# A hybrid mixer and ConvFFN layer on one Trainium2 core: the mixers' projections as pairs with seven half-width block products for eight, the values first, feed-forward operands loaded early

## The chip, the core and the metric

The kernel runs as one program on one core of a Trainium2 chip. Its time is the device time of one execution in microseconds (us); the median of several runs is compared. A core has TensorE (PE, matmuls), VectorE (DVE), ScalarE (ACT), GpSimd (POOL) and SyncE (SP), which here issues all the DMA transfers. Each engine works through its own queue in order, and semaphores tie the queues together.

## The reference, cut to what matters

One layer over 2048 prompt positions and 64 sample positions, all in float32, with D = 1024:

```python
def mixer(xn, ...):
    z = xn @ w_in
    bg, cg, h, q, k, v, gr, r = jnp.split(z, SPLITS, axis=-1)   # 512,512,512,256,256,512,16,512
    cv, conv_new = causal_dwconv(cg * h, conv_prev, conv_w)     # 3 taps
    y_conv = rmsnorm(bg * cv, g_conv)
    logg = jax.nn.log_sigmoid((gr @ w_alpha + b_alpha)) / GATE_TAU
    ...                                                         # q scaled by HEAD_K ** -0.5
    o, gla_new = gla(q, k, v, logg, gla_prev)                   # gated linear attention, chunks of 64
    y_gla = rmsnorm(o, g_gla) * jax.nn.silu(r)
    y = jnp.concatenate([y_conv, y_gla], axis=-1) @ w_out
def conv_ffn(xn, prev, w_up, conv_w, w_down):
    uc, new = causal_dwconv(xn @ w_up, prev, conv_w)            # 1024 -> 2 * 2816, 3 taps
    a, g = jnp.split(uc, 2, axis=-1)
    return (jax.nn.silu(g) * a) @ w_down, new
x = x + mixer(rmsnorm(x)); x = x + conv_ffn(rmsnorm(x)); y = rmsnorm(x)
```

## The kernel before

Positions are the columns of PE's moving operands. They lie in three blocks: 768, 768, and 512 prompt positions with a gap of two and the 64 sample positions (580 columns in all). Half a block is 384, 384 or 290 columns (HALF, CMAX is the largest), and a block has 6, 6 and 5 token tiles of 128 (TILES). A float32 product is made of three matmuls (`product`, L1429; lines L1434 to L1436): every operand is split into a high part, which ACT copies in PE's rounding, and a low part, which is the subtraction raw − high; high·high, high·low and low·high are summed in PSUM.

All three blocks go through the mixer first, then all through the feed-forward part. For each block:

- **Norm and transposes.** Token tiles are normed (x_n), transposed on PE (`turn_1`) and split into xt_hi (ACT) and xt_lo (DVE): 8 k-tiles by the block's columns.
- **First stage ("z").** A unit is 128 output columns of w_in, 512 KB, loaded into one of four slots of `raw`; ACT writes its high part (`high_unit`, L478), POOL its low part (`low_unit`, L485). There are 4 units of r, the gate gr (32 rows, w_gr), and 4 of q and k. Each is computed in two chunks, 256 and 512 (324) columns wide (Z_CHUNKS), in PSUM banks in turn; ACT reads each bank (`read_group`). SiLU of r is applied in gla_y right after the r units.
- **Values.** v_tok is computed by token tile, 24 matmuls of 512 columns each, with the normed positions as weights' side; the weights lie in all four slots. ACT reads them (L1220).
- **Convolution stage.** 12 units (cg, h, bg for j = 0 to 3), each 2 × 24 matmuls of half a block. ACT reads cg into conv_y, DVE multiplies h by it into conv_u, applies three taps, and multiplies by bg. Between these 24 products `mix_events` (L488) deals the steps X, Y and Z of each token tile's linear attention evenly: X makes the state's addends and the output of the first chunk and the next tile's gate, Y the second chunk and the gate's cumulative sum, Z the mean squares and the next tile's scores. Between X and Y, DVE brings the state on (gla_s) and ACT and DVE make the log gate lg, for which PE waits in Y.
- **Out-projection** in four passes p = 0 to 3 over the token tiles, summed on DVE into resid (`add_out`); in pass 3 the second norm and the transposes of the feed-forward operands of this block and of the first norm of the next block run along. The feed-forward operands go to DRAM: parts of the positions (xs_a, xs_b) as x_ops (ops_stored) and four sums of them, made on DVE in tst, from block 0 and 1 (sums_stored).

The feed-forward part has 22 steps for each block. Its up-projections already run as Strassen-Winograd products: a pair of 128-column units as a 2 × 2 block matrix (k halves × units) against the positions as 2 × 2 blocks (k halves × column halves) needs seven half-width products for eight. Sums of the weights (`sum_up`: four of 128 × 512 on DVE), copies on ACT (`high_up`, into slots of wq) and lows on POOL (`low_up`, L906) precede them; r_1, r_2, r_3 are partial results in SBUF. The operands on the positions' side are loaded raw as xo_raw, copied high and subtracted low, 4 × 384 columns each (DVE L1839 in block 0, ACT L1038). In block 0 the split weights are stored to w_ops (L598) for the other blocks.

Each engine's program is written out in order; a load on SP waits until its slot is free, and whatever stands behind it in SP's queue waits too.

## Time and profile before

| | |
|---|---|
| median of 3 runs | 2422.65 us (2420.15 to 2423.34) |
| the profiled execution | 2420.94 us, span 2419.2 us, granted clock 0.992 |
| PE busy | 2320.1 us, 96% |
| DVE, ACT, POOL busy | 1586.5 us, 975.5 us, 1142.3 us |
| mixers of the three blocks, from the timeline | about 18 to 958 us |
| feed-forward part | about 958 us to the end |

A timeline's row gives the start, the length, the engine, the line and the operation, output<-inputs with their shapes, and how many like instructions follow each other (x4). In brackets stands the engine's idle time just before it and the instruction that ended it.

### The profile page before, as it was taken

The numbers are of one execution on the slowest core, as the hardware profiler recorded it, in microseconds if no ns is written. First come the engines' busy times: TensorE is split into PE (matmuls) and PEld (weight loads), VectorE is DVE, ScalarE is ACT, GpSimd is POOL, SyncE is SP. The second block draws the span as 40 slices with busy tenths as digits, with TensorE's granted clock in tenths as the row PEclk, the third lists the DMA queues.
The fourth block names the chain that finished last, engine by engine and source line by source line (L and its number), as shares of the span: only waits on it lengthen the run. The fifth ranks groups of instructions, "written<-read, shape, count | busy, mean of one in ns | idle before, by whom it ended". The sixth has DMA issues, their size and how long they took to land. (4 is left out here: it accounts for less than half of the span.)

```text
span 2419.2 us, 38967 instructions
## 1 busy us (share of the span) xinstructions
PE 2320.1 (96%) x12962; PEld 2113.1 (87%) x12962; DVE 1586.5 (66%) x2397; ACT 975.5 (40%) x1881; POOL 1142.3 (47%) x1117
## 2 busy tenths in 40 slices
PE   7999999999999999799999998999999988999997
PEld 6889878899788987799999998899999987999996
DVE  2046662155650656698988988667667677878886
ACT  4333353333353435444444445333333335444443
POOL 3222323222423334778878785444444445455552
PEclk9999999999999999899999999999999999999999
DMA  5111335111452234744444457644444456555553
GB/s 158 59 53 44 122 114 172 50 44 42 151 183 78 79 120 147 272 170 150 162 173 147 165 175 258 206 160 144 141 160 150 139 183 231 196 191 191 186 195 106
DMA packets 257550, 355.01 MB, mean 147 GB/s; under 512 B 12189, under 2 KB 195314, under 8 KB 257458
## 3 DMA queue, kind: packets, MB, share of 16 engines
q1 hardware_dynamic: 257457, 353.77, 43.8%
q8 instruction: 59, 0.97, 0.2%
q14 instruction: 34, 0.27, 0.0%
HBM read 276.54 MB, written 77.19 MB: 146 GB/s over the span
## 5 line engine op out<-in xcount | busy, mean ns | idle before, releaser
L1434 PE MATMUL ps<-xo,wq 128*128 128x384 f32 (+1 forms) x1848 | 599.7, 324 | 27.6 <-issue 12.0
L1435 PE MATMUL ps<-xo,wq 128*128 128x384 f32 (+1 forms) x1848 | 598.6, 324 | 0.0
L1436 PE MATMUL ps<-xo,wq 128*128 128x384 f32 (+1 forms) x1848 | 598.0, 324 | 0.0
L2089 DVE TENSOR_TENSOR resid<-resid,ps 128x512 f32<-128x512 f32 (+1 forms) x728 | 477.2, 680 | 76.1 <-PE ps L1436 45.3
L485 POOL TENSOR_TENSOR w_lo<-raw,w_hi 128x512 fp32r<-128x512 f32 x192 | 251.4, 1337 | 566.5 <-ACT w_hi L478 566.5
L906 POOL TENSOR_TENSOR wq<-wu_raw,wq 128x256 fp32r<-128x256 f32 x396 | 378.2, 978 | 118.2 <-ACT wq L1018 118.2
L1434 PEld LDWEIGHTS ps<-xo,wq 128*128 128x128 f32 x1848 | 350.4, 190 | 50.5 <-issue 28.0
L1435 PEld LDWEIGHTS ps<-xo,wq 128*128 128x128 f32 x1848 | 351.0, 190 | 20.1
L1436 PEld LDWEIGHTS ps<-xo,wq 128*128 128x128 f32 x1848 | 351.3, 190 | 0.0
L1434 PE MATMUL ps<-xt_hi,w_hi 128*128 128x384 f32 (+4 forms) x960 | 316.7, 330 | 7.9 <-DVE xt_lo L1807 3.7
L2106 DVE SCALAR_TENSOR_TENSOR up_y<-up_u,params,up_y 128x768 f32<-128x768 f32 (+1 forms) x264 | 287.3, 1088 | 50.2 <-ACT up_y L1062 31.5
L1435 PE MATMUL ps<-xt_hi,w_lo 128*128 128x384 f32 (+4 forms) x960 | 310.1, 323 | 0.0
L1436 PE MATMUL ps<-xt_lo,w_hi 128*128 128x384 f32 (+4 forms) x960 | 310.1, 323 | 0.0
L1434 PE MATMUL ps<-wd_hi,hid_hi 128*128 128x512 f32 x704 | 276.8, 393 | 11.7 <-DVE resid L2089 11.6
L1436 PE MATMUL ps<-wd_lo,hid_hi 128*128 128x512 f32 x704 | 277.3, 394 | 0.0
L1435 PE MATMUL ps<-wd_hi,hid_lo 128*128 128x512 f32 x704 | 274.7, 390 | 0.0
L936 POOL TENSOR_TENSOR wd_lo<-wd_raw,wd_hi 128x512 fp32r<-128x512 f32 x132 | 174.7, 1345 | 157.0 <-ACT wd_hi L1097 157.0
L1434 PEld LDWEIGHTS ps<-xt_hi,w_hi 128*128 128x128 f32 x960 | 182.2, 190 | 20.1 <-issue 8.8
L930 POOL TENSOR_TENSOR hid_lo<-up_y,hid_hi 128x384 fp32r<-128x384 f32 (+1 forms) x132 | 120.2, 932 | 165.2 <-ACT hid_hi L1090 165.2
L906 POOL TENSOR_TENSOR wq<-wu_sum,wq 128x256 fp32r<-128x256 f32 x176 | 158.6, 926 | 64.7 <-ACT wq L1018 63.7
L1435 PEld LDWEIGHTS ps<-xt_hi,w_lo 128*128 128x128 f32 x960 | 182.3, 190 | 5.4 <-issue 0.5
L1436 PEld LDWEIGHTS ps<-xt_lo,w_hi 128*128 128x128 f32 x960 | 182.0, 190 | 5.1
(207 smaller groups left out, 3499.2 us busy)
## 6 DMA issues: line engine op xcount, KB each, us to landing
wq<-w_ops SPq DMA_DIRECT2D x176, 512.0 KB, 4.4
wu_raw<-in_w_up_dram SPq DMA_DIRECT2D x89, 512.0 KB, 4.1
w_ops<-wq SPq DMA_DIRECT2D x88, 512.0 KB, 2.7
raw<-in_w_in_dram SPq DMA_DIRECT2D x72, 512.0 KB, 3.9
wd_raw<-in_w_down_dram SPq DMA_DIRECT2D x66, 512.0 KB, 5.1
x_in<-in_x_prompt_dram SPq DMA_DIRECT2D x32, 512.0 KB, 4.5
raw<-in_w_out_dram SPq DMA_DIRECT2D x24, 512.0 KB, 3.4
wu_raw<-in_w_up_dram SPq DMA_DIRECT2D x43, 256.0 KB, 3.1
```

The lines of the kernel that those rows point to most:

```text
L485: last = pool.tensor_tensor(w_lo[:, s, r], raw[:, s, r], w_hi[:, s, r].bitcast(F32), ALU.subtract)
L906: last = pool.tensor_tensor(wq[:, WQ_AT[i], 1, r], src[:, r], wq[:, WQ_AT[i], 0, r].bitcast(F32), ALU.subtract)
L930: last = pool.tensor_tensor(hid_lo[:, par, r], up_y[:, 0, r], hid_hi[:, par, r].bitcast(F32), ALU.subtract)
L936: last = pool.tensor_tensor(wd_lo[:, par, r], wd_raw[:, r], wd_hi[:, par, r].bitcast(F32), ALU.subtract)
L1434: pe.matmul(out, lh, rh, start=(first and n == 0), stop=False, skip_group_check=skip)
L1435: pe.matmul(out, ll, rh, start=False, stop=False, skip_group_check=skip)
L1436: last = pe.matmul(out, lh, rl, start=False, stop=end, skip_group_check=skip)
L2089: last = dve.tensor_tensor(resid[0:m, t, s], resid[0:m, t, s], ps[0:m, bank, :], ALU.add)
L2106: dve.scalar_tensor_tensor(y, up_u[:, m, tap:tap + w], params[:, FFN_TAP + tap, bass.ds(m * NF + f, 1)], y, ALU.mult, ALU.add).then_inc(su ...
```

## The change

It alters the mixers of all three blocks and the hand-over to the feed-forward part; the 66 feed-forward steps stay, apart from the first one's loads.

1. **Values first.** In each block the values are computed straight after the norm, tile 0 and 1 in two halves by weight slots, then the gate product in two chunks of half a block.
2. **Pairs.** r, q and k, cg, h and bg are computed as ten pairs of units (PAIRS), each in seven products of 12 matmuls on half a block (`pair_product`), by the feed-forward part's scheme and with its buffers wu_raw, wu_sum, wq and its semaphores (STEPS = 30 counts lie ahead of the feed-forward part's). Operands 0, 2, 5, 6 are quarters of xt_hi and xt_lo; 1, 3 and 4 are sums of quarters: t_2 and t_3 (DVE) and t_1 (POOL). Operand 5's quarter is also replaced: DVE writes a sum (n4, in xt_raw, which lies over xt_lo's second part) and ACT and DVE split it in place, after the values and the gate product have read the old one.
3. Per pair DVE makes four weight sums, r_2, r_3m and three quarters of the output (four where h and bg are multiplied in), ACT seven copies of weights, r_1 and one quarter, POOL seven lows of 2 × 256 columns; DVE makes the lows 2 and 4 of pairs 1 to 3. For cg, h and bg two convolution rows are handled at once (conv_u0, conv_u1).
4. **Attention steps** begin after product 2 of pair 4; the first tile's gate, sums and scores stand behind products (1, 6), (3, 1) and (4, 2), and 5 products come after the last step. The factor 1/8 of q moves from ACT's read into a DVE operation of each tile. SiLU of r comes after product 2 of pair 2.
5. **Start of the feed-forward part.** Operands 0 to 2 of the positions are loaded at the start of the last block's out stage, 3 and 4 in its middle, 5 and 6 ahead of the last stores to x_ops; their splitting on ACT and DVE moves up as well, and so does the first step's weights'. load_up(0, 1) no longer waits for the stores.
6. Buffers move in SBUF to make place; the parameters' rows are transposed in pair 0 of block 0 instead of in the norm.

```diff
+PAIRS = [("r", 0), ("r", 2), ("qk", 0), ("qk", 2)] + [(kind, j) for j in (0, 2) for kind in ("cg", "h", "bg")]
...
+AT_GATE, AT_SUMS, AT_SCORES = (1, 6), (3, 1), (4, 2)
...
+LEFT = 5
+LOW_PAIRS, LOW_OPS = (1, 2, 3), (2, 4)
...
+        def pair_operand(b, i, part):
+            c = HALF[b]
+            if i in (1, 3, 4):
+                return {1: t_2, 3: t_3, 4: t_1}[i][:, part, :, 0:c]
+            k, c0 = {0: (0, 0), 2: (4, 0), 5: (0, c), 6: (4, c)}[i]
+            return (xt_hi, xt_lo)[part][:, k:k + 4, c0:c0 + c]
```

Order of work (`mix_events`), the loads on SP and the first loads for the feed-forward part:

```diff
-            groups = [(j, m, c) for j in range(CJ) for m in range(3) for c in range(len(CHUNKS[b]))]
+            products = [(p, i) for p in range(NPAIR) for i in range(NP)]
             steps = [(s, t) for t in range(TILES[b]) for s in ("XYZ" if tile_cols(b, t)[1] == P else "XZ")]
-            out, g = [], 0
+            out, g = [], products.index(AT_SCORES) + 1
+            for p, i in products[:g]:
+                out.append(("G", p, i))
+                if (p, i) in (AT_GATE, AT_SUMS, AT_SCORES):
+                    out.append(({AT_GATE: "P", AT_SUMS: "S", AT_SCORES: "C"}[p, i], 0))
+            rest = len(products) - g - LEFT
...
-                upto = (n + 1) * len(groups) // len(steps)
-                while g < upto:
-                    out.append(("G",) + groups[g])
-                    g += 1
-            return out
+                upto = len(products) - LEFT - rest + (n + 1) * rest // len(steps)
+                out += [("G",) + product for product in products[g:upto]]
+                g = upto
+            return out + [("G",) + product for product in products[g:]]
...
+            def load_pair(b, p, part):
+                n = (A11, A21)[part]
+                sp.dma_start(wu_raw[:, n:n + 2, :].rearrange("p n (k c) -> p (n k) c", c=P),
+                             pair_source(p, part)).then_inc(mix_sems[f"w_loaded{part}"], 16)
...
+                unit_free(sp, (0, 1), unit_index(b, "v", 0, 0) + 1)
+                for p in range(NPAIR):
+                    for part in range(2):
+                        if p:
+                            pair_split(sp, NPAIR * b + p - 1, (2, 5)[part])
+                        load_pair(b, p, part)
...
+                if b == NB - 1:
+                    sp.wait_ge(ops_stored, 16 * 3 * b)
+                    sp.wait_ge(sums_stored, 16 * 4 * b)
+                    mix.wait(sp, "p_done", NP * NPAIR)
+                    for i in range(3):
+                        load_x_op(0, i)
+                for n in range(4, 8):
+                    load_unit(sp, out_unit(b, n))
...
-                    sp.wait_ge(ops_stored, 16 * 3 * b)
+                    mix.wait(sp, "out_done", 4 * nt)
+                    for i in range(3, 5):
+                        load_x_op(0, i)
+                    unit_free(sp, (0, 1), unit_index(NB, "v", 0, 0))
                     load_up(0, 0)
...
-                    mix.wait(sp, "out_done", 4 * nt)
-                    for i in range(3):
-                        if i == 2:
...
-                    for i in range(3, 5):
+                    for i in range(5, NP):
                         load_x_op(0, i)
...
-                    sp.wait_ge(ops_stored, 16 * (3 * NB + 1))
-                    for i in range(5, NP):
-                        load_x_op(0, i)
...
+                    sp.wait_ge(ops_stored, 16 * (3 * NB + 1))
                     load_down(0)
```

POOL's t_1 and ACT's order at the start of the pairs:

```diff
+                n1.wait(pool, "lo", 2 * nt)
+                wait(pool, sums_stored, 16 * 4 * b)
...
+                for step, (left, left_part, right, right_part, op) in enumerate([
+                        (xt_hi, c, xt_hi, 0, ALU.subtract), (None, 0, xt_lo, c, ALU.add), (None, 0, xt_lo, 0, ALU.subtract)]):
+                    mix.wait(pool, "t1_step", step)
+                    for k in range(4):
+                        a = left[:, k, left_part:left_part + c].bitcast(F32) if left else t1[:, k]
+                        last = pool.tensor_tensor(t1[:, k], a, right[:, k, right_part:right_part + c].bitcast(F32), op)
+                    mix.inc(last, "t1_step")
...
+                for n in range(nt - 4 if b == 0 else 0, nt):
+                    read_values(n)
+                    if n == 3:
+                        high_sum(1)
+                        high_sum(3)
+                    if n == 4:
+                        high_sum(4)
+                high_pair(NPAIR * b, 0)
+                high_pair(NPAIR * b, 1)
+                for n, (c0, w) in enumerate(CHUNKS[b]):
+                    mix.wait(act, "g_done", n + 1)
+                    mix.inc(act.activation(gate_in[:, c0:c0 + w], ps[0:2 * RANK, (B_GATE, 2)[n], 0:w], ACT.Copy), "g_read")
+                    high_pair(NPAIR * b, 2 + n)
+                high_sum(5)
+                high_pair(NPAIR * b, 4)
+                high_pair(NPAIR * b, 5)
```

PE, values to pairs:

```diff
+                parts = [(0, (0, 1)), (1, (0, 1)), (0, (2, 3)), (1, (2, 3))] + [(n, range(SLOTS)) for n in range(2, nt)]
+                for g, (n, slots) in enumerate(parts):
+                    values(n, slots)
...
+                for n, (c0, w) in enumerate(CHUNKS[b]):
+                    if n:
+                        mix.wait(pe, "v_read", max(i for i in range(nt) if i % 3 == 2) + 1)
...
+                    pair_split(pe, s, i)
+                    if p == 0 and i in (1, 3, 4, 5):
+                        mix.wait(pe, "t_lo", (1, 3, 4, 5).index(i) + 1)
+                    if i == 0:
+                        mix.wait(pe, "c11_read", p)
+                        mix.wait(pe, "v_read", nt)
...
+                    if i == 2:
+                        mix.wait(pe, "r1_read", p + 1)
+                    if i == 3:
+                        mix.wait(pe, "r2_read", p + 1)
+                    if i == 4:
+                        mix.wait(pe, "c12_read", p)
+                        mix.wait(pe, "g_read", nch)
...
+                    mix.inc(product(ps[:, bank, 0:c], [
+                        (wq[:, WQ_AT[i], 0, k * P:(k + 1) * P], wq[:, WQ_AT[i], 1, k * P:(k + 1) * P],
+                         hi[:, k], lo[:, k]) for k in range(4)], first=i in (0, 1, 4), skip=True), "p_done")
```

DVE's sums of the positions (the five first and three last steps):

```diff
+                operand_step(0, 3, b22, b12[0], ALU.subtract)
+                operand_step(1, 3, t_raw, b22_l, ALU.add)
+                operand_step(2, 3, t_raw, b12[1], ALU.subtract)
+                operand_step(3, 1, t_raw, b11, ALU.add)
+                operand_step(4, 1, t2_raw, b11_l, ALU.add)
+                pair_sums(0)
+                operand_low(1, 1)
+                operand_low(2, 3)
+                operand_low(3, 4)
+                mix.wait(dve, "v_done", nt)
+                mix.wait(dve, "g_done", nch)
+                mix.wait(dve, "t_lo", 3)
+                t2, n4_raw = high_low(1), unsplit(b, 5)
+                operand_step(5, 5, b21, t2[0], ALU.subtract)
+                operand_step(6, 5, n4_raw, b21_l, ALU.add)
+                operand_step(7, 5, n4_raw, t2[1], ALU.subtract)
+                operand_low(4, 5)
```

The order on the engines, at three places. First ACT in block 0, before, from the end of the r units to the first q and k units (gate_in is the gate, qk the queries and keys, w_hi the high part of a unit's weights):

```order
L1124 ACTIVATE gate_in_86<-ps 32x256 [waits mix_z_done]
L1124 ACTIVATE gate_in_86<-ps 32x512 [waits mix_z_done]
L1129 ACTIVATE qk_81<-ps 128x256 [waits mix_z_done]
L1129 ACTIVATE qk_81<-ps 128x512 [waits mix_z_done]
L478 ACTIVATE w_hi_62<-raw_69 128x1024 [waits raw_ready0]
L1129 ACTIVATE qk_81<-ps 128x256 [waits mix_z_done]
```

After, from the last but one token tile's values to the first pair (wq are high parts of the pair's weights, wu_sum their sums, xt_hi<-xt_raw the sum n4):

```order
L1172 ACTIVATE v_tok_76<-ps 128x512 [waits mix_v_done]
L1181 ACTIVATE t_1_105<-t_1_raw_106 128x1536 [waits mix_t1_step]
L1172 ACTIVATE v_tok_76<-ps 128x512 [waits mix_v_done]
L1193 ACTIVATE wq_64<-wu_raw_129 128x512 [waits mix_w_loaded0]
L1193 ACTIVATE wq_64<-wu_sum_128 128x512 [waits mix_w_summed]
L1221 ACTIVATE gate_in_90<-ps 32x384 [waits mix_g_done]
L1193 ACTIVATE wq_64<-wu_raw_129 128x512 [waits mix_w_summed,mix_w_loaded0]
L1221 ACTIVATE gate_in_90<-ps 32x384 [waits mix_g_done]
L1193 ACTIVATE wq_64<-wu_sum_128 128x512 [waits mix_w_summed]
L1181 ACTIVATE xt_hi_67<-xt_raw_70 128x4x384 [waits mix_t_step]
...
L1303 ACTIVATE r_1_65<-ps 128x384 [waits mix_p_done]
```

The copy of t_1 stands between two reads of values, and the copy of n4 and four copies of weights stand ahead of r_1.

POOL in block 0, before, in the first stage:

```order
L485 TENSOR_TENSOR w_lo_63<-raw_69,w_hi_62 128x512
L868 MEMSET q_exp_90 128x512 [waits first_turned]
L869 MEMSET k_end_t_93 128x512
L870 MEMSET att_94 128x512
L485 TENSOR_TENSOR w_lo_63<-raw_69,w_hi_62 128x512 [waits hi_ready3]
```

and after, between the values' weights and the first pair's:

```order
L908 MEMSET q_exp_94 128x512 [waits first_turned]
L909 MEMSET k_end_t_97 128x512
L910 MEMSET att_98 128x512
L924 TENSOR_TENSOR t_1_raw_106<-xt_hi_67 128x384 [waits first_lo]
L924 TENSOR_TENSOR t_1_raw_106<-xt_hi_67 128x384 x3
L924 TENSOR_TENSOR t_1_raw_106<-t_1_raw_106,xt_lo_68 128x384 [waits mix_t1_step]
...
L924 TENSOR_TENSOR t_1_raw_106<-t_1_raw_106,xt_lo_68 128x384 [waits mix_t1_step]
...
L494 TENSOR_TENSOR wq_64<-wu_raw_129,wq_64 128x256 [waits mix_w_hi]
L494 TENSOR_TENSOR wq_64<-wu_raw_129,wq_64 128x256
L494 TENSOR_TENSOR wq_64<-wu_sum_128,wq_64 128x256 [waits mix_w_hi]
```

Twelve subtractions and additions for t_1 have come between the clearing of buffers and the first low of the pairs.

PE in block 0 around one token tile's attention, before (L1551 begins step X, L1565 Y, L1573 Z; each L1434 here begins 24 matmuls):

```order
L1551 MATMUL ps<-v_tok_82,k_end_t_93 128x128 [waits mix_state1,mix_state0,mix_gla_y,mix_att_read,mix_turned_read]
...
L1516 MATMUL ps<-w_al_104,gate_in_86 128x256 [waits mix_turned_read]
L1434 MATMUL ps<-xt_hi_67,w_hi_62 128x384 [waits mix_cg_read,lo_ready2]
...
L1565 MATMUL ps<-q_exp_90,gla_s_102 128x2x64 [waits mix_state0]
...
L1522 MATMUL ps<-tri_100,lg_87 128x128 [waits mix_lg]
...
L1434 MATMUL ps<-xt_hi_67,w_hi_62 128x384 [waits mix_u_done]
...
L1573 MATMUL ps<-o_sq_95,ones_101 128x512 [waits mix_o_rs,mix_o_squared]
L1530 MATMUL ps<-q_exp_90,k_exp_91 128x128 [waits mix_att_read,mix_qk_exp]
...
L1434 MATMUL ps<-xt_hi_67,w_hi_62 128x384 [waits mix_u_done,lo_ready0]
```

and after (L1695 X, L1709 Y, L1717 Z; each L1543 begins a product of 12 matmuls):

```order
L1695 MATMUL ps<-v_tok_76,k_end_t_97 128x128 [waits mix_state1,mix_state0,mix_gla_y,mix_att_read,mix_turned_read]
...
L1660 MATMUL ps<-w_al_115,gate_in_90 128x256 [waits mix_turned_read]
L1543 MATMUL ps<-t_2_74,wq_64 128x384 [waits mix_c21_read,pair_low_p,pair_low_v]
...
L1543 MATMUL ps<-xt_hi_67,wq_64 128x384 [waits mix_r1_read,pair_low_p,pair_low_v]
...
L1709 MATMUL ps<-q_exp_94,gla_s_113 128x2x64 [waits mix_state0]
...
L1666 MATMUL ps<-tri_111,lg_91 128x128 [waits mix_lg]
...
L1543 MATMUL ps<-t_3_69,wq_64 128x384 [waits mix_r2_read,pair_low_p,pair_low_v]
...
L1543 MATMUL ps<-t_1_105,wq_64 128x384 [waits mix_c12_read,mix_g_read,pair_low_p,pair_low_v]
...
L1717 MATMUL ps<-o_sq_99,ones_112 128x512 [waits mix_o_rs,mix_o_squared]
L1674 MATMUL ps<-q_exp_94,k_exp_95 128x128 [waits mix_att_read,mix_qk_exp]
...
L1543 MATMUL ps<-xt_hi_67,wq_64 128x384 [waits mix_r3_read,pair_low_p,pair_low_v]
```

Between two steps stand two products of 12 matmuls where one of 24 (two behind Z) stood, and the products' waits are now for r_1, r_2 and the lows of the weights.

## Rows read from the trace of the kernel before

**Rows 1.** The page, part 1: busy time of PE and the other engines.
```profile
PE 2320.1 (96%) x12962; PEld 2113.1 (87%) x12962; DVE 1586.5 (66%) x2397; ACT 975.5 (40%) x1881; POOL 1142.3 (47%) x1117
```
**Rows 2.** PE's timeline in block 0: a first-stage unit, two value tiles, a convolution unit.
```profile
65.03 0.28 PE L1434 MATMUL ps<-xt_hi,w_hi 128*128 128x256 f32 x1
...
73.38 0.28 PE L1434 MATMUL ps<-xt_hi,w_hi 128*128 128x256 f32 x1
...
105.02 0.50 PE L1434 MATMUL ps<-w_hi,xt_hi 128*128 128x512 f32 x1
...
116.04 0.60 PE L1522 MATMUL ps<-tri,lg 128*128 128x128 f32 x4
...
149.55 0.42 PE L1434 MATMUL ps<-xt_hi,w_hi 128*128 128x384 f32 x1
...
157.99 1.05 PE L1551 MATMUL ps<-v_tok,k_end_t 128*128 128x128 f32 x8
```
**Rows 3.** PE's timeline in block 2: a first-stage unit.
```profile
739.06 0.28 PE L1434 MATMUL ps<-xt_hi,w_hi 128*128 128x256 f32 x1
...
745.52 0.28 PE L1434 MATMUL ps<-xt_hi,w_hi 128*128 128x256 f32 x1
```
**Rows 4.** PE's timeline at the program's start: two of the waits.
```profile
18.08 0.55 PE L1434 MATMUL ps<-xt_hi,w_hi 128*128 128x256 f32 x1 [1.99 <-DVE xt_lo L1807]
...
37.65 0.47 PE L1434 MATMUL ps<-xt_hi,w_hi 128*128 128x512 f32 x1 [1.67 <-DVE xt_lo L1807]
```
**Rows 5.** Windows (stretch, busy by engine, PEclk, DMA share, GB/s): feed-forward start.
```profile
958.00:980.00 22.00, 14.38 (x60) 13.46 (x61) 11.84 (x14) 10.11 (x12) 8.51 (x10) 0.77 0.92 315
980.00:1003.00 23.00, 15.38 (x68) 14.35 (x67) 13.26 (x16) 11.23 (x20) 19.36 (x20) 0.85 0.89 329
```
**Rows 6.** PE's timeline there: the two longest waits.
```profile
974.10 0.66 PE L1434 MATMUL ps<-xo,wq 128*128 128x384 f32 x1 [5.03 <-issue]
...
988.73 0.66 PE L1434 MATMUL ps<-xo,wq 128*128 128x384 f32 x1 [4.25 <-ACT r L1024]
```
**Rows 7.** Timeline of ACT and DVE: copies and lows of the shapes that are added.
```profile
941.36 0.61 ACT L1018 ACTIVATE wq<-wu_raw 128x512 fp32r<-128x512 f32 x1
...
946.03 1.49 ACT L1038 ACTIVATE xo<-xo_raw 128x1536 fp32r<-128x1536 f32 x1
...
954.50 1.74 DVE L1839 TENSOR_TENSOR xo<-xo_raw,xo 128x1536 fp32r<-128x1536 f32 x1
...
955.67 0.50 ACT L1024 ACTIVATE r<-ps 128x384 f32<-128x384 f32 x1
```
**Rows 8.** POOL's line L919 (ns min/median/max): subtractions of 384 and 290 columns.
```profile
L919 POOL TENSOR_TENSOR xo<-xo_raw,xo x16: 803/1022/1737, 1469.0 to 1998.9; 128x384 fp32r<-128x384 f32 x8, 128x290 fp32r<-128x290 f32 x8
```
**Rows 9.** Timeline: DVE beside POOL and alone, then POOL beside DVE and alone.
```profile
363.60 1.79 DVE L2038 TENSOR_TENSOR tst<-xs_a 128x512 f32<-128x512 f32 x1
...
370.98 0.68 DVE L2039 TENSOR_TENSOR tst<-xs_b,xs_a 128x512 f32<-128x512 f32 x1
...
963.04 2.77 POOL L906 TENSOR_TENSOR wq<-wu_sum,wq 128x256 fp32r<-128x256 f32 x2 [1.84 <-ACT wq L1018]
965.78 1.41 POOL L906 TENSOR_TENSOR wq<-wu_raw,wq 128x256 fp32r<-128x256 f32 x2
```
**Rows 10.** SyncE's timeline: stores of block 0's sums (tst) at block 1's start.
```profile
375.55 3.06 SPq L739 DMA_DIRECT2D x_ops<-tst  x4
```
**Rows 11.** Windows, columns as in rows 5: block 0's convolution stage.
```profile
134.00:272.00 138.00, 134.48 (x814) 128.13 (x813) 76.29 (x171) 50.50 (x101) 39.32 (x30) 1.00 0.19 56
```
**Rows 12.** DVE's timeline in one token tile: from the state to the log gate.
```profile
183.88 1.41 DVE L1918 SCALAR_TENSOR_TENSOR gla_s<-gla_s,decay,ps 64x128 f32<-64x128 f32 x4 [8.27 <-PE ps L1558]
...
187.14 0.42 DVE L1887 SCALAR_TENSOR_TENSOR lg<-lg,soft 128x256 f32<-128x256 f32 x1 [1.38 <-ACT soft L1171]
```
**Rows 13.** The page, part 6 (KB each, us to landing): loads of a pair's weights.
```profile
wu_raw<-in_w_up_dram SPq DMA_DIRECT2D x89, 512.0 KB, 4.1
```
**Rows 14.** The page, part 5 (busy, mean ns): POOL's lows of feed-forward weights.
```profile
L906 POOL TENSOR_TENSOR wq<-wu_raw,wq 128x256 fp32r<-128x256 f32 x396 | 378.2, 978 | 118.2 <-ACT wq L1018 118.2
```

882 lines of the change are left out of this document (491 added, 391 removed).

## The prediction

> **What bounds the kernel now.** I read the page's busy shares first: TensorE (PE) is busy 2320.1 of 2419.2 us [rows 1], so the program lasts as long as its matmuls and the 99 us in which PE stands. Then the timeline of PE, for what one product costs in each stage of a mixer [rows 2, 3]; then what ended PE's idle times, which lie at the program's start [rows 4] and at the start of the feed-forward part [rows 5, 6]. In the mixer stage that the change rewrites, 134.48 of 138.00 us are busy [rows 11]: only 3.5 us stand there in block 0. So a product less is a product's time less, if its operands come in time, and every new wait of PE is added whole. The question is what the seven-product form asks of DVE, ACT and POOL before and between the products.
>
> **The change, part by part; the sum is made against the profiled span of 2419.2.** The profiled execution took 2420.94, 1.7 over its span, and the median of the runs is 2422.65, again 1.7 above that; so the median is the span plus 3.4.
>
> 1. Fewer products. In blocks 0 and 1 a unit of the first stage (a 256 and a 512 wide chunk) takes 73.38 − 65.03 = 8.35 us, and one of the convolution stage (48 matmuls of 384) 157.99 − 149.55 = 8.44, or 0.176 a matmul [rows 2]. Eight of the one and twelve of the other: 168.1. The new form has 10 pairs × 84 matmuls × 0.1758 = 147.7, so 20.4 less in each of the two. In block 2 a unit of 580 columns takes 6.46, or 0.1346 a matmul [rows 3]: 20 × 6.46 = 129.2 against 840 × 0.1346 = 113.1, 16.1 less. The values (5.5 a tile, 11.02 for two [rows 2]) and the gate are only moved. **−57.0.**
>
> 2. Program start and the first stage's small waits. The first product starts at 18.08 after a wait of 1.99, and the wide chunk waits 1.67 at 37.65 for the last token tiles, both for xt_lo [rows 4]. Values by token tile need one tile at a time, so 3.5 goes there and some slow clock with it; the parameter transposes leave this part for pair 0. **−8.5** in all blocks together, of which the two waits carry 3.7 and the rest is estimated; between −4 and −12.
>
> 3. Start of the feed-forward part. PE is busy 14.38 of 22.00 us and 15.38 of 23.00 [rows 5]: 15.2 stand. The granted clock is 0.77 and 0.85 there, between its two levels of 1.2 and 2.4 GHz; half speed for 46% and 30% of the time, which costs another 5 and 3.5. Two waits alone are 5.03 and 4.25 [rows 6]: the operands of products 3 to 6 are loaded behind stores of other operands on SyncE's queue. The change loads operands 0 to 4 in the out stage and lifts load_up(0, 1) and operands 5, 6 from behind the wait for the stores. Not all of the 23.7 goes, since the DMA share is 0.92 and 0.89 [rows 5] and the bytes are the same; a third is taken. **−8**, between −4 and −14.
>
> 4. Start of the pairs, once in each block. This is new.
>    (a) ACT copies t_1's high part between two reads of values. The second gate chunk (blocks 0 and 1) or product 0 (block 2) waits for the last of these reads, so PE waits for POOL's t_1. It is 12 operations of 384 columns: 0.80 at best and 1.02 in the mean [rows 8]. DVE works at the same time on five sums and two lows of 1536 columns at 1.74 [rows 7] and four weight sums of 0.68 [rows 9], 14.9 in all. The two take turns: a DVE operation of 512 columns took 1.79 while POOL ran and 0.68 alone, and POOL's own 1.41 became 2.77 beside DVE [rows 9]. Block 0's last token tile is ready at 37.6 [rows 4]; 37.6 + 14.9 + 12 × 1.02 + 1.49 and 0.50 for ACT [rows 7] = 66.7. PE is through six tiles (33), four transposes (about 4), the slow start (about 2) and chunk 1 (16 × 0.176) at about 60. So 7 in block 0; 4 if POOL's operations take their least. In block 1 t_1 overlays what the last block's sums are stored from, and these stores are issued from 375.55 to 378.61 [rows 10], when PE is already in the block's first products; landed some us later, they let POOL start while PE has about 20 us of values left, against 12.2 to 27.1 of t_1 and its turns and 2 of ACT. I take 5.5 between 1 and 10, and in block 2, which has a tile less of values on fewer columns, 6.5 between 4 and 9. **+19.**
>    (b) t_2, t_3 and t_1 are covered by values, but the fourth sum may be written only when the gate product has been read out of xt_lo: its three steps (5.2), its copy (1.49), three copies of weights queued on ACT ahead of r_1 (1.8) and r_1's own 0.50 [rows 7] stand before product 2 of pair 0; only products 0 and 1 (4.2) cover them. 4.8, 4.8, and in block 2 on 290 columns 4.0; one turn with POOL's low, 1.41 [rows 9], in each. **+18**, up to 26.
>    (c) The first weight sums wait for a load behind the values' slots: 1 a block, **+3**. (d) After long waits PE's clock falls: it costs 8.5 beside the 15.2 that PE stands in [rows 5], where two waits are over 4; with one or two such waits a block I take 2 each, **+6**.
>
> 5. Among the steps of linear attention. Before, 24 products of 4.22 are dealt to 17 gaps, 6.0 each; now a gap holds two of 2.11. DVE's chain from the state to the log gate that PE waits for is 187.14 + 0.42 − 183.88 = 3.7 [rows 12], without any of the pair's work ahead of it; now up to four weight sums (2.7) and a quarter (0.5) may be queued in front. Walking DVE's and ACT's queues through block 0 gives waits of 2 to 5 us at the third step of the first tiles and at the last tile's, 1 elsewhere, 13 in all if each meeting with POOL costs a whole turn, where 3 stand today; 10 more a block. With half the turns it is 6.7. **+20**, between 10 and 45. The attention steps themselves, the queries' scale that moves to DVE and the SiLU at another place: 0, they lie under products.
>
> Sum: −57.0 − 8.5 − 8 + 19 + 18 + 3 + 6 + 20 = **−7.5**. Span 2411.7, median **2415**.
>
> **The rivals.**
> - *The fill is hidden.* If POOL's t_1 runs at 0.80 with few turns, part (a) falls to 9, (b) to 14, (d) to nothing and the attention gaps to +10: −73.5 + 9 + 14 + 3 + 10 = −37.5, 2385; with one of them at the middle, **2393**. For it: DVE is busy 76.29 of 138 in this stage and POOL 39.32 [rows 11]. Against it: both work at once just at a block's start.
> - *The weights come too slowly*: **slower than before**. A pair's second load waits for the low of the last pair's product 5. From there: load 4.1 [rows 13], four sums, ACT's copy 0.61 [rows 7], five lows. At 0.68 and 1.41 that is 14.6. A block-0 pair with its share of attention takes 7 × 2.11 + 7 = 22, a block-2 pair 7 × 1.61 + 7 = 18.3, a pair without attention 14.8. The same kind of low takes 2 × 0.978 = 1.96 in the mean of the feed-forward part [rows 14], so the loop is 4.1 + 4.4 + 0.6 + 9.8 = 18.9 there: it decides in block 2 from a low of 1.85 on. At 2.5 a low and 1.2 a sum it is 22.0: 3.6 × 9 pairs of block 2 and 7 × 2 at the bare pairs, +46: **2461**.
>   For this the row with DVE's 1.79 against 0.68 speaks [rows 9]. The Trainium skill, page "SBUF — State Buffer", section "SBUF: two separate sides", says that DVE operations with two SBUF inputs and GpSimd's share a port pair as an exclusive lock held for the whole instruction; the trace agrees (1.79 against 0.68). By that rule every sum and every POOL low meet whole, and the time would lie near 2461; without it near 2393.
> - *Turns all round, no loop*: (a) 29, (b) 26, attention +31: **2444**.
> - *The early loads bring nothing*, since DMA is as full in the out stage once they lie there: part 3 at 0, **2423**, no change.
>
> **How the numbers follow.** Forecast (own range 2400 to 2426, in which its faster, same and slower parts are 0.29, 0.08 and 0.05) 0.42; fill hidden 0.20; weights too slow 0.17; turns all round 0.15; early loads bring nothing 0.06. 0.2% is about what a measurement of this kernel can tell from no change, 4.8 us. Faster 0.49, same 0.13, slower 0.38. The range must reach from the hidden fill to the turns and near the loop: 2383 to 2460.
>
> **What would show it.** PE has 360 matmuls fewer and its busy time falls by about 57. Step 4: in each block one wait of PE at the second gate chunk or product 0, put down to ACT's read or POOL, of 4 to 10 us, and one of 5 to 9 at product 2 of pair 0, put down to r_1; none would mean the hidden fill. Step 5: waits of products for r_1, r_2 or the quarters of some 1 us, under 10 a block. The loop would show as waits of PE for POOL's low of the weights, in block 2 above all. Step 3: 958 to 1003's waits must be gone by a third to a half. It would be wrong if attention gaps stand for 15 a block, or if a granted clock below 1 runs through whole pairs.

## The result: 2483.8 us, slower by 2.6%

| | before | after |
|---|---|---|
| median | 2422.53 us (2420.15 to 2423.34) | 2483.77 us (2482.26 to 2491.15) |
| ratio of the two | | 1.0261 (95%: 1.0239 to 1.0282) |
| profiled execution's span | 2419.2 us | 2481.9 us |
| PE busy, granted clock | 2320.1 us, 0.992 | 2296.9 us, 0.974 |

Each median is of four executions. The forecast was 2415, with a range that ended at 2460. The page after, part 1, against [rows 1]:

```profile
PE 2296.9 (93%) x12602; PEld 2089.5 (84%) x12602; DVE 1833.3 (74%) x2673; ACT 1046.5 (42%) x2037; POOL 1365.7 (55%) x1423
```

There are 360 matmuls less, but PE's busy time falls by 23 and not by 57, mostly since more of them run at the lower of the two clock levels: counted from the granted clock over PE's busy time, the slow clock costs 42.5 us now and 13.4 before. And PE now stands 185 us of the span where it stood 99. DVE is busy 247 us more, POOL 223; part of this is no new work, since operations of the two last longer beside each other (below).

To see where, I split the span at places that both kernels have: the first gate product, the first step X of the attention, the start of the out-projection, in each block. In each stretch PE's **work** is the sum of its matmuls at the median pitch of their form at full clock; what the stretch is longer than that is **lost**: as standing, as slow clock, or in matmuls that last longer than their median though the clock is full. Another way of taking the pitch moves single figures by up to 5 us and the differences between the two kernels by up to 2. The sums over the three blocks:

| us lost | before | after | more | forecast |
|---|---|---|---|---|
| program's start to block 0's gate (first 13 us apart) | 8.7 | 4.2 | −4.5 | −8.5 |
| gate to first step X (pairs 0 to 4 after; gate, q, k, values before) | 8.4 | 77.9 | +69.5 | +46 |
| attention, to the out-projection | 19.2 | 60.2 | +41.0 | +20 |
| out-projection to the next gate, or feed-forward part | 30.1 | 50.0 | +19.9 | 0 |
| feed-forward part | 64.6 | 59.8 | −4.8 | −8 |
| work in all | 2266.0 | 2206.1 | −59.9 | −57 |

With +0.9 in the first 13 us this gives +62.1 to the last matmul, and the spans differ by 62.7. The products' gain came whole. It was spent two times over in the mixers.

What is more in a mixer stretch can be taken apart further, since the trace has PE's idle times and the granted clock: from the gate to the first step X PE stands 53.1 us more and the slow clock costs 14.5 more, in the attention 25.7 and 11.4, in the out stage 13.3 and 5.9.

**The waits of PE**, the longest in the list of waits after (us in total, times, longest):

```profile
PE ps L1617 <- ACT v_tok L1172: 18.5, 2, 9.9
PE ps L1553 <- DVE x_n L1913: 18.0, 12, 8.5
PE ps L1543 <- issue: 16.6, 6, 11.6
PE ps L1543 <- ACT r L1303: 11.3, 3, 5.7
PE ps L1695 <- DVE gla_y L2100: 10.7, 5, 3.4
PE ps L1543 <- DVE resid L2256: 10.6, 6, 3.9
```

L1617 is the gate product, L1303 the copy of r_1. On PE's timeline these waits lie at the starts of block 0, block 1 and block 2:

```profile
65.36 0.53 PE L1617 MATMUL ps<-xt_hi,w_gr 128*32 128x384 f32 x1 [8.59 <-ACT v_tok L1172]
80.33 0.66 PE L1543 MATMUL ps<-xt_hi,wq 128*128 128x384 f32 x1 [5.69 <-ACT r L1303]
...
422.72 0.53 PE L1617 MATMUL ps<-xt_hi,w_gr 128*32 128x384 f32 x1 [9.90 <-ACT v_tok L1172]
437.91 0.66 PE L1543 MATMUL ps<-xt_hi,wq 128*128 128x384 f32 x1 [5.42 <-ACT r L1303]
...
770.88 0.58 PE L1543 MATMUL ps<-xt_hi,wq 128*128 128x290 f32 x1 [11.61 <-issue]
788.13 0.58 PE L1543 MATMUL ps<-xt_hi,wq 128*128 128x290 f32 x1 [4.31 <-DVE gla_y L2117]
```

The first four are the two waits of step 4 of the forecast, at the places that it named: the second gate chunk and product 2 of pair 0. Block 2 went another way. ACT and POOL there:

```profile
755.00 0.60 ACT L1172 ACTIVATE v_tok<-ps 128x512 f32<-128x512 f32 x1 [0.82 <-PE ps L1545]
765.82 1.17 ACT L1181 ACTIVATE t<-t_raw 128x1160 fp32r<-128x1160 f32 x1 [10.22 <-POOL t_raw L924]
...
767.59 3.19 POOL L494 TENSOR_TENSOR wq<-wu_raw,wq 128x256 fp32r<-128x256 f32 x2 [1.80 <-ACT wq L1193]
```

The last values were read at 755.00, before t_1's copy and not behind it, since block 2 has five token tiles. Product 0 starts at 770.88, 0.1 us after POOL has made the low of the first weights; this low stands behind t_1 on POOL, and the copy that it needs behind t_1's copy on ACT. So the wait is t_1's, by a path that the forecast didn't name. For r_1 PE stood only 0.2 there, and the 4.31 is for a quarter, of which more under e6. Matmuls of 384 columns take 0.66 behind the waits, where they take 0.41 at full clock. Block 0's attention and out stage, after, and then the latter before (columns as in [rows 5]); the first line answers to [rows 11]:

```profile
149.59:280.15 130.56, 121.07 (x705) 112.77 (x705) 98.20 (x200) 59.60 (x126) 64.69 (x74) 0.96 0.22 69
280.15:409.87 129.72, 115.92 (x532) 92.71 (x533) 90.47 (x105) 56.70 (x102) 47.71 (x35) 0.97 0.42 140
```

```profile
271.98:394.73 122.75, 114.56 (x581) 94.01 (x582) 75.80 (x94) 57.35 (x105) 43.14 (x29) 1.00 0.51 167
```

The windows that answer to [rows 5], moved by the 68.76 us that the feed-forward part starts later, show 12.4 us of standing for 15.2 and a clock of 0.92 and 0.78 for 0.77 and 0.85:

```profile
1026.76:1048.76 22.00, 17.23 (x90) 16.11 (x91) 8.71 (x12) 9.68 (x14) 9.75 (x12) 0.92 0.89 296
1048.76:1071.76 23.00, 15.38 (x64) 13.94 (x63) 14.81 (x17) 10.66 (x19) 19.12 (x21) 0.78 0.83 300
```

The wait of 5.03 for the loads [rows 6] is gone; one of 4.98 for r_1 is still there, where one of 4.25 stood. Counted as the forecast counts it, the clock costs 6.8 in these windows for 8.5.

### The profile page after: what moved, and what is told of

It reads as the page before. It is cut to its first block and busy times, and to the rows that moved or that the text cites. A ratio compares the mean times of both kernels' runs of the same rounds, so it can differ in the third digit from the quotient of the medians.

```text
span 2481.9 us, 39628 instructions
## 1 busy us (share of the span) xinstructions
PE 2296.9 (93%) x12602; PEld 2089.5 (84%) x12602; DVE 1833.3 (74%) x2673; ACT 1046.5 (42%) x2037; POOL 1365.7 (55%) x1423
## 5 line engine op out<-in xcount | busy, mean ns | idle before, releaser
L1543 PE MATMUL ps<-xo,wq 128*128 128x384 f32 (+1 forms) x1848 | 599.2, 324 | 23.3 <-ACT r L1079 5.3
L1543 PEld LDWEIGHTS ps<-xo,wq 128*128 128x128 f32 x1848 | 349.9, 189 | 46.3 <-issue 16.9
L494 POOL TENSOR_TENSOR wq<-wu_sum,wq 128x256 fp32r<-128x256 f32 x222 | 191.0, 882 | 241.1 <-ACT wq L1193 240.6
L1543 PE MATMUL ps<-wd_hi,hid_hi 128*128 128x512 f32 x704 | 276.0, 392 | 10.4 <-DVE resid L2333 10.4
L1543 PE MATMUL ps<-xt_hi,wq 128*128 128x384 f32 (+1 forms) x480 | 165.6, 345 | 43.5 <-issue 11.6
L961 POOL TENSOR_TENSOR wq<-wu_sum,wq 128x256 fp32r<-128x256 f32 x176 | 159.5, 931 | 70.7 <-ACT wq L1073 70.7
L1543 PE MATMUL ps<-w_hi,xt_hi 128*128 128x512 f32 (+1 forms) x408 | 167.2, 410 | 22.0 <-DVE resid L2256 10.6
L1117 ACT ACTIVATE up_y<-up_u,params 128x768 f32<-128x768 f32 (+1 forms) x132 | 116.9, 886 | 120.0 <-DVE up_u L2441 81.9
L1545 PE MATMUL ps<-w_lo,xt_hi 128*128 128x512 f32 (+1 forms) x408 | 161.8, 397 | 0.0
L1544 PE MATMUL ps<-w_hi,xt_lo 128*128 128x512 f32 (+1 forms) x408 | 161.8, 396 | 0.0
L1544 PE MATMUL ps<-xt_hi,wq 128*128 128x384 f32 (+1 forms) x480 | 159.7, 333 | 0.0
```

What stands on the lines that cost most here:

```text
L494: last = eng.tensor_tensor(wq[:, at, 1, r], w[:, r], wq[:, at, 0, r].bitcast(F32), ALU.subtract)
L961: last = pool.tensor_tensor(wq[:, WQ_AT[i], 1, r], src[:, r], wq[:, WQ_AT[i], 0, r].bitcast(F32), ALU.subtract)
L1117: return act.activation(up_y[:, m, 0:w], up_u[:, m, 2:2 + w], ACT.Copy, scale=params[:, FFN_TAP + 2, bass.ds(m * NF + f, 1)])
L1543: pe.matmul(out, lh, rh, start=(first and n == 0), stop=False, skip_group_check=skip)
L1544: pe.matmul(out, ll, rh, start=False, stop=False, skip_group_check=skip)
L1545: last = pe.matmul(out, lh, rl, start=False, stop=end, skip_group_check=skip)
```

## Why the blocks start late

Block 0, DVE's first operand sums, and POOL's t_1 beside them:

```profile
39.27 2.60 DVE L1995 TENSOR_TENSOR t_raw<-xt_hi 128x1536 f32<-128x1536 f32 x1
41.91 4.94 DVE L1995 TENSOR_TENSOR t_raw<-t_raw,xt_lo 128x1536 f32<-128x1536 f32 x2
```

```profile
39.25 8.47 POOL L924 TENSOR_TENSOR t_raw<-xt_hi 128x384 f32<-128x384 f32 x4
47.79 15.51 POOL L924 TENSOR_TENSOR t_raw<-t_raw,xt_lo 128x384 f32<-128x384 f32 x8
```

Taken singly, a POOL operation lasts 2.4 to 2.5 us beside DVE's of 1536 columns, 1.3 to 1.5 beside DVE's weight sums of 512 columns, and 1.0 while DVE idles (four in 3.94 at 404.21, below). A DVE operation of 1536 columns lasts 2.45 instead of 1.76, a sum 1.4 to 1.5 instead of 0.69. From 39.3 to 63.3 DVE makes eleven operations and POOL twelve: they alternate one by one. t_1 is ready at 63.3; the forecast had 64.7 before ACT's copy. Block 0 went as the sum said (8.6 and 5.7 for 7 and 6).

Block 1: SyncE's stores of the sums and the loads of the first pair's weights behind them, then POOL and DVE:

```profile
389.01 5.23 SPq L789 DMA_DIRECT2D x_ops<-tst  x4
394.35 5.34 SPq L644 DMA_DIRECT2D wu_raw<-in_w_in_dram  x2
```

```profile
404.21 3.94 POOL L924 TENSOR_TENSOR t_raw<-xt_hi 128x384 f32<-128x384 f32 x4 [17.13 <-issue]
...
407.60 1.12 DVE L2012 TENSOR_TENSOR wu_sum<-wu_raw 128x512 f32<-128x512 f32 x1 [4.05 <-DMA wu_raw<-in_w_in_dram]
```

The stores go out at 389.01 and not at 375.55 [rows 10], 13.5 us later, though block 1's first product starts only 4.5 later (366.50 for 361.98); DVE writes the last of the sums at 388.15 for 374.83. They also take 7.4 to 11.1 us to land, for 3.3 to 9.1 before. Why DVE is so late isn't taken apart. POOL starts t_1 at 404.2, with values for only 5.7 us left on PE, and not for 20 as the forecast took from the rows of before. The weights load behind the same stores, so DVE's sums meet POOL's t_1 too.

## The experiments

The columns of the table at the end of this section are the three mixer stretches from above, and what PE stood in the attention. Unless an interval is given, a run's figures are those of one execution, beside ones of the kernel before at 2420 to 2422. Executions of one kernel differ: 23 of the kernel before lay between 2416.1 and 2425.5, four of the changed one between 2482.3 and 2491.2. A difference under some 5 us therefore says nothing by itself, and neither does one of 4 or 5 us in a stretch that the edit doesn't touch: the attention lost 4.2 more in e1, 3.4 more in e123 and 4.9 more in q1, all with the standing unchanged within 1.5 us. It is the slow clock that differs there. What PE stands in a stretch repeats better, and the readings below go by it where they can.

**e1, values read first.** ACT's copy of t_1 goes behind the reads of the values:

```diff
-                    if n == 4:
-                        high_sum(4)
+                high_sum(4)
```

> ACT copies t_1's high part after all reads of the values instead of ahead of the last one; nothing else moves. Theory T (POOL's t_1 itself is the long thing, since DVE and POOL take turns; it ends at 63.3 in block 0 and the first pair's lows stand behind it on POOL): the second gate chunk no longer waits (8.6 and 9.9 before), but the first product of the pairs waits in its place; only the chunk's own 2.8 us is won in blocks 0 and 1, nothing in block 2, so the span falls by 5 to 10 us, to 2472 to 2477. Rival R (the order on ACT is the cause): the three waits of 8.6, 9.9 and 11.6 go, and the clock's loss with them: 2445 to 2455.

2482.7, span 2481.0, 0.9 less. The wait moved, as theory T has it, to the first product of the pairs, behind POOL's lows. The 5 to 10 us that T promised came only where the edit is (5.0 less lost to the first step X); the slow clock of the attention took them back. PE's timeline in block 0:

```profile
69.22 0.69 PE L1542 MATMUL ps<-xt_hi,wq 128*128 128x384 f32 x1 [9.93 <-POOL wq L494]
```

**e2, r_1 before n4.**

```diff
-                high_sum(5)
-                high_pair(NPAIR * b, 4)
-                high_pair(NPAIR * b, 5)
...
+                        if not p:
+                            for n in (4, 5, 6):
+                                high_pair(s, n)
+                            high_sum(5)
```

> The copy of r_1 and the sum r_2 are put ahead of the splitting of the fourth operand (n4) in pair 0 of each block. If r_1's place behind n4's copy causes the 5.7, 5.4 us waits at product 2: products 2 to 4 come before n4 is needed, the waits go down to under 1 in blocks 0 and 1, about 5 in each, and with the clock that stays up 12 to 18 us in all: 2464 to 2470. If instead the sums and lows of pair 0's weights are late as well, the wait moves to products 3 to 5 and the span falls by under 5.

2476.0, 7.7 less, half of what was expected, and only 3.3 of it before the first step X; most of the rest is the attention's clock. The wait of 5.69 is gone, but one of 4.37 for a quarter came eight microseconds later. DVE stood for the next pair's weights and then made their sums, and the quarter lay behind both:

```profile
84.94 0.69 DVE L2014 TENSOR_TENSOR wu_sum<-wu_raw 128x512 f32<-128x512 f32 x1 [4.16 <-DMA wu_raw<-in_w_in_dram]
...
87.48 0.55 DVE L2118 TENSOR_TENSOR gla_y<-ps,r_3m 128x384 f32<-128x384 f32 x1
88.18 0.66 PE L1545 MATMUL ps<-xt_hi,wq 128*128 128x384 f32 x1 [4.37 <-DVE gla_y L2118]
```

**e8, no operand sums.** Products 1, 3, 4 and 5 read plain quarters; steps, copies and lows are out.

```diff
-                return {1: t_2, 3: t_3, 4: t_1}[i][:, part, :, 0:c]
-            k, c0 = {0: (0, 0), 2: (4, 0), 5: (0, c), 6: (4, c)}[i]
+            k, c0 = {0: (0, 0), 2: (4, 0), 5: (0, c), 6: (4, c), 1: (4, 0), 3: (0, 0), 4: (0, c)}[i]
```

> Leaves out part of the computation: the sums of the positions' quarters (t_1, t_2, t_3 and n4, their copies and lows) are not made, products 1, 3, 4 and 5 multiply plain quarters instead; products, weights' sums and everything between the attention steps are as in the changed kernel. If the preparation of these operands is what PE stands for at each block's start, the lost time between the gate product and the first attention step (23.0, 23.2 and 31.7 us in the three blocks) falls by 17 to 20 in each and the span to 2423 to 2432. If the load and the sums of the first pair's weights are as late as the operands, a wait of 5 to 10 us stays in blocks 1 and 2 and the span falls to 2440 to 2450 only.

2434.7, span 2432.8: **the preparation of the operands costs 49 us.** The window of block 0 from the gate to the first step X now holds 2.5 us of standing in 77.3, at full clock:

```profile
53.60:130.90 77.30, 74.78 (x434) 70.40 (x432) 33.90 (x57) 35.80 (x66) 45.07 (x60) 1.00 0.25 69
```

In block 2 21 us stay lost even so. Without any preparation of operands the new form is still 14 us behind the kernel before, so the start of the blocks is not the whole cause.

**e123, t_1 on DVE**, with the moves of e1 and e2 (three operations of 1536 columns for POOL's twelve).

```diff
+                for n, (left, right, op) in enumerate([(b12[0], b11, ALU.subtract), (t1, b12[1], ALU.add), (t1, b11_l, ALU.subtract)]):
+                    mix.wait(dve, "t1_step", n)
+                    mix.inc(dve.tensor_tensor(t1, left, right, op), "t1_step")
```

> Three moves together: ACT reads all values before it copies t_1; r_1 and r_2 go ahead of n4's splitting; and t_1 is made by DVE in three operations of 1536 columns instead of POOL's twelve. If turns between DVE and POOL set the block's start, DVE's operations fall back from 2.45 to 1.74 us; its eleven operations and the weight sums then take about 22 us from the last token tile on, where t_1 was ready after 24, and the weights' lows no longer stand behind t_1: the lost time at the start of each block falls by 8 to 12 us, the span to 2443 to 2455. If it is the length of DVE's queue alone, t_1 comes no earlier and the gain is that of the two moves, some 8 us: 2472 to 2476.

2464.1, 19.7 less, and DVE's sums are back at their own time:

```profile
39.36 1.76 DVE L1988 TENSOR_TENSOR t_raw<-xt_hi 128x1536 f32<-128x1536 f32 x1
41.15 3.55 DVE L1988 TENSOR_TENSOR t_raw<-t_raw,xt_lo 128x1536 f32<-128x1536 f32 x2
```

So the turns are shown at the start of the block: with more work on DVE and none of t_1 on POOL, t_1 is ready at 53.5 for 63.3. Lost to the first step X: 54.4 for 77.9, 23.5 less where 24 to 36 were expected. The span came out at 2462.3, 7 above the stated range; 3.4 of these are the attention's, in the same run. The move of t_1 brings some 11 us beyond e1 and e2. It does two things at once, it ends the turns with t_1 and it lets the weights' lows on POOL start at 56.8 for 65.9; which share each has isn't separated.

**e4, short lows, and e5, short sums**: which of the two fills the attention part?

```diff
-                r = slice(n * 512 // parts, (n + 1) * 512 // parts)
+                r = slice(n * 512 // parts, n * 512 // parts + (512 // parts if s % NPAIR == 0 or parts == 1 else 32))
```

> Leaves out part of the computation: POOL's lows of the weights of pairs 1 to 9 are made on 2 x 32 of 2 x 256 columns (the rest of each slot is old data), so POOL is nearly free after pair 0. Theory T (DVE and POOL take whole turns, and POOL's lows stretch DVE's work among the attention steps and the weight loop): PE's lost time in the attention part falls from 14.8 to 7 us in block 0 and in block 2 from 28 to under 14, the span by 25 to 35 us: 2447 to 2457. Rival Q (DVE's own queue is too long, whatever POOL does): under 10 us.

```diff
+                    if p:
+                        a0, a1, g0, g1, s1, s2, s3, s4 = (v[:, 0:64] for v in (a0, a1, g0, g1, s1, s2, s3, s4))
```

> Leaves out part of the computation: DVE's four weight sums of pairs 1 to 9 are made on 64 of 512 columns, which takes about 2.2 us (5 beside POOL) from DVE in each pair; POOL's lows stay. Theory T (turns): the sums are the DVE operations that meet POOL's lows most, so the lost time in the attention part falls by 10 to 15 us in all, less than with POOL's lows short. Rival Q (DVE's queue): it falls by 20 to 35 us, more than with the short lows. The wait for the load of the weights ahead of the sums stays in both, so block 2's waits of 4.3, 2.4 and 2.5 at products 6 stay.

2474.1 and 2447.0: 9.6 less without most of POOL's lows, 36.6 less without most of DVE's weight sums, 23 of these in the attention part and 11 ahead of it. By their stated bounds rival Q holds: what DVE has in its queue is the larger part, and my theory, that the turns are the main thing everywhere, fell. But the turns are not nothing. With the short lows the attention part alone lost 14.2 less (7.4 of it standing), with the short sums 23.0 (13.1 standing); a sum that is nearly gone meets no low either, so the two gains overlap and can't be added. (What goes to the first step X rose by 2.3 with the short lows.) Against what was expected, block 2's waits behind the load shrank too with the short sums, from 6.7 and 4.1 us to 4.1 and 0.4.

**e6, sums behind the quarter**: `pair_sums(p + 1)` moves from product 3 to behind the quarter of product 4. In the changed kernel's block 2 DVE waits at the load, with two quarters behind it:

```profile
784.99 0.69 DVE L2012 TENSOR_TENSOR wu_sum<-wu_raw 128x512 f32<-128x512 f32 x1 [3.90 <-DMA wu_raw<-in_w_in_dram]
...
787.53 0.46 DVE L2117 TENSOR_TENSOR gla_y<-ps,r_3m 128x290 f32<-128x290 f32 x1
```

> DVE makes the next pair's four weight sums after the quarter of product 4 instead of ahead of it, so a late load of weights no longer holds that quarter, for which product 6 waits. If the waits of 4.3, 2.4, 2.5 and 1.6 us in block 2 are this queueing and nothing else, they shrink to under 1 each and the span falls by 8 to 12 us. If they are the loop from the low of product 5 over the load, the sums and the lows to the next pair's products, later sums make it longer: no gain, or up to 10 us slower, with waits put down to POOL's lows (line 494).

2482.9, 0.7 less. Both happened: 11.4 less lost ahead of the attention (8.0 of it in block 2), 11.2 more in it. The second rival's loop is there in its first half: in the changed kernel the load of pair 1's second half is issued at 781.15, 0.07 us after POOL has made the low of product 5, and DVE's first sum starts when it has landed, at 784.99. But PE waited for a quarter behind the sums in DVE's queue, and not for the lows at the loop's end. In e6 the waits for lows that the rival gave as its sign are only 2.0 and 1.9 us; what grew in the attention is the wait for DVE's k_end, from 10.1 to 17.2, behind the sums again.

**p1, the first pair plain.** If sums of positions can't be ready in time, the first pair can do without them: r 0 and 1 as eight plain half-products (two of them in one), no weight sums, n4 made while they run, t_1 on DVE, first weights loaded ahead of the stores. Its table of slot, k half, column half and bank:

```diff
+HALVES = [(3, 0, 1, 0, 0), (4, 4, 1, 0, 0), (5, 0, 1, 1, 1), (6, 4, 1, 1, 1), (3, 0, 0, 2, 2), (4, 4, 0, 2, 2), (5, 0, 0, 0, 3)]
```

> A fix of the block's start. The first pair (r 0, 1) is computed as eight plain half-width products of quarters (two of them as one of 24 matmuls) without weight sums, so the sums of the positions are needed one pair later; t_1 is made on DVE, n4 while the plain pair runs, and the first pair's weights are loaded ahead of the stores to x_ops. It costs one half product more a block, 2.1, 2.1 and 1.6 us. If the preparation of the operands (49 us by the run without it) can be covered by 17 us of products, the lost time between the gate product and the first attention step falls from 23.0, 23.2 and 31.7 to 6, 6 and 15 to 20 and the span to 2440 to 2448. If the work only moves (DVE is full there in any case and is late at the second pair or at the first gate step), it stays above 2458, the value of the three moves without it.

> As the run before, and DVE makes the next pair's weight sums behind the quarter of product 4 for pairs 0 to 3 only, ahead of the attention steps; later pairs as in the changed kernel. The move for all pairs gave 1.7, 1.7 and 8.0 us before the first attention step and took 1.4, 1.9 and 7.8 in the attention part; so the early pairs alone should give 8 to 11 us: 2430 to 2438. If the 7.8 were carried over from the early pairs, it gives under 3.

> As the run before with both r pairs plain: another 5.8 us of products in all, and four weight sums, three copies and three lows less in pair 1, and the sums of the positions needed one pair later still. If one plain pair covers the preparation, this one is slower by 3 to 6 us; if DVE is still late in pair 1, it is faster by 3 to 10.

2443.2, 2431.8 and 2441.2; the first two lie where they were expected. Against the changed kernel p1 brings 40.6; of these 19.7 are e123's moves, which it contains, and 20.9 the plain pair with its earlier weights. The later sums for early pairs bring 11.4 more. What is lost to the first step X is 17.2, of which 10.6 in block 2. A second plain pair costs 9.4 where 3 to 6 were expected, 5.8 of it as products; it brings nothing.

**q1, q2, q3, the out stage and the attention.** In the out stage DVE of the run p1e6 waits for x that SyncE loads behind two output weights, and in the changed kernel's block 1 PE waits for the second half of the values' weights:

```profile
276.10 2.60 DVE L2339 TENSOR_TENSOR resid<-ps,x_in 128x512 f32<-128x512 f32 x4 [4.45 <-DMA x_in<-in_x_prompt_dram]
```

```profile
378.65 0.79 PE L1543 MATMUL ps<-w_hi,xt_hi 128*128 128x512 f32 x1 [4.69 <-POOL w_lo L529]
```

```diff
-                for n in range(4, 8):
+                for n in range(4, 6):
                     load_unit(sp, out_unit(b, n))
...
                     load_x_again(t)
+                    if t == 2:
+                        for n in range(6, 8):
+                            load_unit(sp, out_unit(b, n))
...
+                early = 3 if b else 2
```

> As p1e6, with two moves at the out stage, where 20 us more are lost than in the kernel before: SP loads x of token tile 2 ahead of the last two output weights (DVE stood 4.45 us for it, PE 1.55), and in blocks 1 and 2 three instead of two value tiles are begun on the first half of the weights before the second half's lows are needed (PE stood 4.7 us for them). If these two queues are the cause: the lost time between out-projection and next gate falls by 4 to 6 in blocks 0 and 1 and by 3 in block 2's out stage, the span by 8 to 14: 2416 to 2422. If only the first is: 3 to 5 us.

2424.8, 7.1 less, just short of the 8 to 14; the out stage loses 40.0 for 51.4, and the attention 4.9 more, without an edit there and with 1.5 us less of standing.

In the attention part of p1e6, at the fourth tile's step X, DVE's queue and then PE's wait:

```profile
186.83 0.68 DVE L2068 TENSOR_TENSOR wu_sum<-wu_raw 128x512 f32<-128x512 f32 x1
...
189.36 2.91 DVE L2202 SCALAR_TENSOR_TENSOR conv_y<-conv_u,params,conv_y 128x768 f32<-128x768 f32 x2
192.30 0.89 DVE L2143 COPY_PREDICATED att<-tri,ps 128x128 f32<-128x128 uint32 x4
193.10 0.74 DVE L2160 SCALAR_TENSOR_TENSOR o_sq<-ps,params,o_sq 128x512 f32<-128x512 f32 x1
193.88 0.89 DVE L2163 TENSOR_TENSOR gla_y<-gla_y,o_sq 128x512 f32<-128x512 f32 x1
...
194.91 2.04 PE L1746 MATMUL ps<-v_tok,k_end_t 128*128 128x128 f32 x8 [3.43 <-DVE gla_y L2163]
```

Four weight sums and two taps, 5.4 us, stand ahead of the scores and gla_y, though nobody needs them yet. q2 puts them behind:

```diff
-                        if 4 <= p and p + 1 < NPAIR:
+                        if 4 <= p and p + 1 < NPAIR and p != 6:
                             pair_sums(p + 1)
-                        if kind == "bg":
+                        if kind == "bg" and p != 6:
                             conv_taps(u, 1)
...
+                        if p == 6:
+                            conv_taps(u, 1)
                         pair_quarter(p, 1, 1, 2, r_3m, "c22_read")
-                        if p < 4:
+                        if p < 4 or p == 6:
                             pair_sums(p + 1)
```

> As q1, and in pair 6 the convolution taps of the second row and the next pair's weight sums (2.9 and 2.7 us on DVE) come behind the attention's scores and output instead of ahead of them. If DVE's queue order causes the wait of 3.4 us for gla_y at the fourth tile's first step, it goes in blocks 0 and 1, with some clock: 6 to 10 us. If the work is only moved, another step waits as long: within 2 us of q1.

> As q2, with 3 instead of 5 products behind the last attention step, so that each of the 18 gaps in blocks 0 and 1 has two products instead of two gaps with one. If cover is what lacks, 2 to 4 us faster than q2; if the end of the attention (heads' lows for the out-projection) becomes late, 2 to 6 us slower.

2419.5: 5.3 less. The attention parts of blocks 0 and 1 lose 10.1 less than in q1 and 6.2 less than in p1e6, that of block 2 3.0 more; why isn't shown. The wait of 3.43 is gone, with waits of 1.02 for the state and 1.58 for the log gate in its place:

```profile
185.04 0.90 DVE L2147 COPY_PREDICATED att<-tri,ps 128x128 f32<-128x128 uint32 x4 [0.20 <-PE ps L1729]
...
187.36 2.07 DVE L2206 SCALAR_TENSOR_TENSOR conv_y<-conv_u,params,conv_y 128x768 f32<-128x768 f32 x2
...
195.59 0.71 PE L1764 MATMUL ps<-q_exp,gla_s 128*128 128x128 f32 x4 [1.02 <-DVE gla_s L2157]
```

So DVE's order caused the wait, and the work that was moved holds other steps for less. But of the 10.1 only 2.1 are standing; the rest is slow clock, which in p1, with q2's wait of 3.4 still in place, cost as little in these two blocks (1.7 us). What the move is worth in time is therefore not shown beyond some 2 us.

q3 came to 2418.0, with 4.3 more lost in the attention of blocks 0 and 1 (2.8 of it standing; the text ahead of r2 has 2 for the whole): its gain lies in stages that it doesn't touch.

**r1 and r2, all moves together, timed.** q2's taps in blocks 0 and 1 only, and the first half of the convolution's mean of squares one token tile later:

> All moves together, timed: the plain first pair, early pairs' sums later, the out stage's two moves, pair 6's taps behind the scores in blocks 0 and 1 only (in block 2 they cost 3 us), and the mean of squares of the convolution one token tile later in the out-projection (PE stood 1.1 for each). From q2's 2419.5: block 2's 3 us and 2 to 4 for the means, 2413 to 2417, against 2420 to 2423 of the kernel before: faster by 0.2 to 0.35%. If block 2's loss in q2 was not the taps', it stays at 2418 to 2420, the same as before.

> As r1 with 3 products left behind the last attention step instead of 5. q3 against q2 lost 2 us more in the attention parts of blocks 0 and 1 and was faster only by other stages; so 2 to 4 us slower than r1, unless those other stages' gain came with the move, then 1 to 3 faster.

r1: 2418.8 in the median of 12, ratio to the kernel before 0.9993 (0.9984 to 1.0002): **the same**, where 2413 to 2417 were expected. The kernel before had 2421.2 beside it, in the median of 23. r2: 2422.0, 1.0003 (0.9993 to 1.0013), the same too. Against each other r2 is 3.2 slower, as expected, and PE stands 3.5 more in the attention of blocks 0 and 1, as in q3 against q2: three products behind the last step are, if anything, worse than five. Block 2's attention came back only from 27.3 to 24.6, and the later mean was a miss: PE waited longer for it, not less (once 4.3), and the out stage lost 44.2 for q2's 42.3.

| | us | to first X | attention | of it stood | out stage |
|---|---|---|---|---|---|
| before | 2422.5 | 8.4 | 19.2 | 7.5 | 30.1 |
| after | 2483.8 | 77.9 | 60.2 | 33.2 | 50.0 |
| e1 | 2482.7 | 72.9 | 64.4 | 33.1 | 50.0 |
| e2 | 2476.0 | 74.6 | 56.4 | 34.6 | 48.1 |
| e8, operand sums out | 2434.7 | 30.3 | 57.9 | 34.8 | 48.1 |
| e123 | 2464.1 | 54.4 | 63.6 | 33.7 | 49.6 |
| e4, lows short | 2474.1 | 80.2 | 46.0 | 25.8 | 51.1 |
| e5, weight sums short | 2447.0 | 66.7 | 37.2 | 20.1 | 47.5 |
| e6 | 2482.9 | 66.5 | 71.4 | 42.9 | 47.6 |
| p1 | 2443.2 | 36.3 | 55.6 | 33.7 | 46.6 |
| p1e6 | 2431.8 | 17.2 | 59.9 | 34.2 | 51.4 |
| p2e6 | 2441.2 | 18.4 | 61.7 | 34.4 | 51.8 |
| q1 | 2424.8 | 18.3 | 64.8 | 32.7 | 40.0 |
| q2 | 2419.5 | 18.5 | 57.6 | 33.5 | 42.3 |
| q3 | 2418.0 | 18.0 | 60.8 | 34.9 | 39.0 |
| r1 | 2418.8 | 17.9 | 55.3 | 29.9 | 44.2 |
| r2 | 2422.0 | 18.1 | 61.6 | 32.8 | 43.4 |

## Why the prediction was wrong, step by step

The span came out 70.2 us above the forecast's 2411.7. Of these 23.5 are step 4's, 21.0 step 5's, 19.9 the out stage's, 4.0 and 3.2 those of steps 2 and 3, less 2.9 of step 1; 1.5 lie outside these stretches.

- **Step 1, fewer products, right**: −57 forecast, −59.9 measured as work.
- **Step 2, the start**: −4.5 for −8.5, inside its bounds (−4 to −12).
- **Step 3, the feed-forward start**: −4.8 for −8, inside. The loads did come early; the wait for r_1 of 4.98 was not theirs. This part was not undone alone, and it differs by some 5 us between runs whose edits don't touch it, so the −4.8 is not told from nothing.
- **Step 4, the start of the pairs: the waits were there, the size was wrong**, +69.5 for +46. Of this 53.1 is standing, where (a), (b) and (c) have 40, and 14.5 slow clock, where (d) has 6. Block 0 was right within 2 us. The failing term is (a) in blocks 1 and 2, 9.9 and 11.6 for 5.5 and 6.5. In block 1 it took from [rows 10] when the stores of the sums go out, though the change itself puts them 13 us later. In block 2 it had the wrong path: not the last read of values, but the lows of the first weights behind t_1. Term (b) came in blocks 0 and 1 (5.7 and 5.4) and not in block 2 (0.2): 11.3 for 18. Term (c) was one microsecond a block; in block 2 the weight loads held DVE's quarters for 4.3, 2.4, 2.5 and 1.6.
- **Step 5, the attention: mis-sized**, +41 for +20. It lay within its bounds (10 to 45). PE stands 25.7 more, near the forecast's 20. The other large part is 11.4 of slow clock, for which the step has no term at all; (d) stands in step 4 alone. The half of the walk's waits that I took, on the ground that half of the meetings with POOL cost no whole turn, was no bad size. But e4 and e5 show that the turns are the smaller cause of the waits, and what stands in DVE's queue the larger: the sums, and the two taps of 2.9 us, which the step doesn't name.
- **The step that is missing**: the out stage, with +19.9 for 0. The forecast has no term for it, and takes the values as only moved. But this stretch holds the start of the next block, where the values now come first, and PE stood 6.9 for the lows of their weights, for 0.8 before. For DVE's sums into resid it stood 10.6, for 2.9; DVE itself stood 20.8 us there for x from SyncE's queue, for 12.2 before. q1, two edits in orders of queues, gave back 11.4 of it in p1e6. In block 2 the loads that step 3 moves may have a hand in it. The x of the third token tile is issued at 960.50, behind the first operands of the feed-forward part (950.10) and four output weights, 8.8 us after the out-projection's start, for 4.7 before (893.71); DVE and then PE stood for it:

```profile
967.00 2.55 DVE L2256 TENSOR_TENSOR resid<-ps,x_in 128x512 f32<-128x512 f32 x4 [6.58 <-DMA x_in<-in_x_prompt_dram]
967.83 0.66 PE L1543 MATMUL ps<-w_hi,xt_hi 128*64 128x512 f32 x1 [3.87 <-DVE resid L2256]
```

  No run takes these early loads back alone, so their share isn't known. That the out stage's loss comes from the pairs' work in the queues is not shown either: with most weight sums gone (e5) it lost 47.5, for 50.0.
- **The range** ended at 2460. The upper ends that the text has, −73.5 + 29 + 26 + 3 + 6 + 45, give 35.5, or 2458; so it held for these terms all together. What broke it is the missing 19.9 of the out stage and the clock: with these 19.9, and 15 for (d)'s 6, the same ends give 2487. Terms (a) and (c) and the attention came at or near their upper ends or above them at once, where the forecast took their middles; (b) did not.
- **The rivals.** "Weights too slow" was right that the result is slower, and it named block 2, where the first half of its loop was seen; PE's waits there, 10.8 us, were behind it but not at its end, and they are not the main cost. Its page, the Trainium skill's "SBUF — State Buffer", section "SBUF: two separate sides", with its lock for a whole instruction, agrees with the operations at the start of a block (DVE's 2.45 beside POOL's, 1.76 alone). That it would put the time near 2461 wasn't borne out as the cause: with POOL's lows short only 9.6 us come back. "Turns all round" had (a) right (29 for 30.1) and (b) too high (26 for 11.3); it too has no out stage. "The fill is hidden" fell with the waits of 5 to 12 us, and whether the early loads bring anything is open.
- The parts named for the chances add up to 0.14 for the same and 0.37 for slower, where 0.13 and 0.38 stand; nothing hangs on it.

## What to carry to other kernels

Before a product is taken away by making its operands out of others, ask when the first sum can be ready and what covers it; if nothing does, let the first products go without sums (one plain pair in each block, 6 us of matmuls in all, gave back 21 us net here, together with an earlier load of its weights). Then write down each in-order queue at the places where PE waits, with every operation that now stands ahead of what it waits for, also in stages whose own work is unchanged: two changes of order there were worth 11.4 us of their stage. Where the terms of a sum hang on the same busy engine, as here on DVE, expect their errors to add up and not to cancel. And give the slow clock a term in every step that has waits: it was 42.5 us here for 13.4 before, and the forecast had 6.

Here the form can be brought level with the kernel before by order, by t_1's place and by one plain pair a block, 2483.8 to 2418.8, but the 51.8 us less of matmuls that r1 keeps bought nothing: it loses 9.5, 36 and 14 us more than the kernel before in the three mixer stretches, and 10 less at the program's start and in the feed-forward part.

## What I had not expected of the chip

- DVE and POOL do not only slow each other down by some share, they alternate operation by operation: in 24 us twelve operations of POOL stood beside eleven of DVE. A POOL operation of 384 columns took 2.4 to 2.5 us beside DVE's of 1536 columns, 1.3 to 1.5 beside those of 512, and 1.0 alone, and each of DVE's 0.7 to 0.8 longer. A short operation on one engine pays for a long one on the other.
- What the slow clock costs doesn't follow from how long PE stands. Long waits bring it: after, block 0's stretch to the first step X, with its waits of 8.59 and 5.69, stood 17.2 us at a granted clock of 0.91, and the slow part cost 4.1. In r1, where the longest wait in these stretches is 2.0 us, PE stood 11.9 in the three of them at full clock. But the same waits can go either way. In block 0's attention e1 and e2 have the same code, the same longest wait of 3.4 and standing of 10.0 and 10.5 us, and yet:

```profile
146.79:279.54 132.75, 122.74 (x705) 114.44 (x705) 98.77 (x200) 59.48 (x126) 64.59 (x74) 0.95 0.22 68
148.94:276.60 127.66, 117.12 (x704) 109.05 (x705) 98.79 (x200) 59.48 (x126) 64.64 (x74) 1.00 0.23 71
```

  The first line is e1's, at a clock of 0.95, the second e2's, at 1.00: 5.1 us for nothing that either edit does there. A gain of that size in one execution is no evidence for a queue's order; the standing is.
